# The first loads of a two-block transformer kernel issued early, in halves and in order, and the second block's context loaded and prepared sooner

## What is computed

```python
h = rms_norm(x, gain)
proj = jnp.einsum('bsd,de->bse', h, w_in)          # 1024 -> 9808 columns
...                                                 # three attentions: oa, ob, oc, each 512 wide
y = jnp.einsum('nbsw,nwd->bsnd', jnp.stack([oa, ob, oc], axis=0), w_branch)
gates = jax.nn.sigmoid(merge_logit).reshape(B, S, N_BRANCH, D_MODEL)
merged = jnp.sum(gates * y, axis=2)
return x + jnp.einsum('bsd,de->bse', merged, w_out)
```

```python
h   = modulate(x,   norm1_g[layer], sh1, sc1)
h_c = modulate(ctx, norm1_g[layer], csh1, csc1)
y = even_mixer(h, ...)         # layer 0; the same for h_c
...                            # layer 1: neighbourhood attention of x over x and ctx
x = x + g1 * y
x = x + g2 * conv_ffn(modulate(x, norm2_g[layer], sh2, sc2), ...)
```

## Time and profile before

| what | value |
|---|---|
| median of 3 runs | 1578.64 us (1578.16 to 1579.22) |
| the profiled execution | 1579.09 us, its span 1577.3 us |
| PE busy | 1538.7 us, 98% of the span |
| DVE, ACT, POOL busy | 66%, 48%, 6% |
| mean granted TensorE clock | 0.995 |
| moved by DMA | 260.9 MB, mean 165 GB/s |

### The profile page before, as it was taken

The page is one execution under the profiler, slowest core; times in us unless marked ns, Lnnn a source line. Parts: engine busy times, 40 slices in busy tenths (PEclk is TensorE's granted clock), DMA queues, the critical chain, the costliest instruction groups (busy, mean ns, idle before and its releaser), DMA issues.

```text
span 1577.3 us, 31432 instructions
## 1 busy us (share of the span) xinstructions
PE 1538.7 (98%) x13599; PEld 1472.3 (93%) x13599; DVE 1039.6 (66%) x1347; ACT 756.5 (48%) x1132; POOL 100.7 (6%) x79
## 2 busy tenths in 40 slices
PE   5999999999999999999999999999999999989999
PEld 5999999999999999899999999999999996889999
DVE  5878767578877775554456758886345347766674
ACT  4555554465465544653355322233245327655453
POOL 0311000003010000000020000000011002000000
PEclk9999999999999999999999999999999999989999
DMA  7676454566774546512035557754335224245854
GB/s 263 217 242 221 163 178 149 183 228 208 241 241 160 188 161 211 178 64 81 28 108 174 174 180 241 243 179 143 90 116 174 90 81 102 86 134 154 234 172 136
DMA packets 312333, 260.92 MB, mean 165 GB/s; under 512 B 24066, under 2 KB 298498, under 8 KB 312068
## 3 DMA queue, kind: packets, MB, share of 16 engines
q1 hardware_dynamic: 294260, 253.52, 49.6%
q10 hardware_dynamic: 17936, 5.40, 1.6%
HBM read 257.85 MB, written 1.05 MB: 164 GB/s over the span
## 4 chain that ended last, share of the span: by engine, by line
PE 54%; issue 7%; DVE 5%; ACT 3%; DMA 0%; POOL 0%; ACTq 0%; DVEq 0%; SPq 0%; POOLq 0%
PE banks_g L1417 34%; PE banks_g L967 7%; PE banks_g L1127 5%; PE banks_g L1276 2%; DVE w_lo L2498 1%; ACT near_p L2043 1%; DVE w_lo L2200 1%; PE banks_g L956 1%; ACT w_hi L1794 1%; PE banks_g L1378 1%; PE bank_s L1450 0%; POOL bias L2128 0%; PE bank_t L1464 0%; DVE near_max L2792 0%; PE bank_t L894 0%
## 5 line engine op out<-in xcount | busy, mean ns | idle before, releaser
L1417 PE MATMUL banks_g<-h_hi,w_lo 128*128 128x256 f32 x1296 | 360.5, 278 | 1.0 <-DVE w_lo L2498 0.6
L1417 PE MATMUL banks_g<-h_lo,w_hi 128*128 128x256 f32 x1296 | 358.5, 277 | 0.0
L1417 PE MATMUL banks_g<-h_hi,w_hi 128*128 128x256 f32 x1296 | 358.5, 277 | 0.0
L2498 DVE TENSOR_TENSOR w_lo<-raw,w_hi 128x2048 fp32r<-128x2048 f32 (+1 forms) x100 | 207.6, 2076 | 100.6 <-ACT w_hi L1794 100.3
L2200 DVE TENSOR_TENSOR w_lo<-raw,w_hi 128x2048 fp32r<-128x2048 f32 x92 | 212.4, 2310 | 72.5 <-ACT w_hi L1594 72.2
L1417 PEld LDWEIGHTS banks_g<-h_hi,w_lo 128*128 128x128 f32 x1296 | 243.5, 188 | 3.0 <-issue 0.9
L1417 PEld LDWEIGHTS banks_g<-h_hi,w_hi 128*128 128x128 f32 x1296 | 243.6, 188 | 0.0
L1417 PEld LDWEIGHTS banks_g<-h_lo,w_hi 128*128 128x128 f32 x1296 | 243.3, 188 | 0.1
L967 PE MATMUL banks_g<-h_hi,w_lo 128*128 128x256 f32 x800 | 226.0, 283 | 0.3 <-DVE w_lo L2200 0.3
L967 PE MATMUL banks_g<-h_hi,w_hi 128*128 128x256 f32 x800 | 221.4, 277 | 0.0
L967 PE MATMUL banks_g<-h_lo,w_hi 128*128 128x256 f32 x800 | 221.4, 277 | 0.0
(11 more groups left out here) (414 smaller groups left out, 3277.3 us busy)
## 6 DMA issues: line engine op xcount, KB each, us to landing
raw<-w_in SPq DMA_DIRECT2D x76, 1024.0 KB, 4.8
raw<-w_up SPq DMA_DIRECT2D x88, 512.0 KB, 4.9
ada_raw<-ada_w SPq DMA_DIRECT2D x24, 1024.0 KB, 7.1
raw<-w_down SPq DMA_DIRECT2D x32, 704.0 KB, 4.3
raw<-w_branch SPq DMA_DIRECT2D x12, 1024.0 KB, 4.9
ada_raw<-ada_t SPq DMA_DIRECT2D x12, 1024.0 KB, 4.9
late_raw<-ada_t SPq DMA_DIRECT2D x12, 1024.0 KB, 5.0
raw<-qkv SPq DMA_DIRECT2D x12, 1024.0 KB, 4.9
```

Of the source, the lines that this page charges most:

```text
L1417: last = nc.tensor.matmul(to, w[:, c, m0:m0 + P], a[:, c, s_ * SEQ:s_ * SEQ + SEQ], start=(m, s_, c, n) == (0, 0, 0, 0), stop=(m, s_, c, n ...
L2498: nc.vector.tensor_tensor(w_lo[:, u % SLOTS, 0:n], raw[:, u % SLOTS, 0:n], w_hi[:, u % SLOTS, 0:n].bitcast(F32), ALU.subtract).then_inc(dv ...
```

## The change

At the start ACT issues `ident` and `vectors`, with a counter of their own. SP issues `x` in two halves by features, unit 0 in two halves by chunks, unit 1, `ada` 0, unit 2, `w_small`, the six constants and unit 3, and waits for nothing before these. ACT makes the small columns for `ada` (`s_f`, `s_cols`) first, then two banks of `o_hi`, half of unit 0, two banks, the other half, then the sums of squares of x by rows from `x_in` with its accumulator, then unit 1. DVE reads the banks for `o_lo` itself, takes `w_lo` of unit 0 in two halves, and copies x to `x_t` afterwards. In layer 0 PE makes one matmul in place of the 8 of `sumsq`, and the root is taken from ACT's own sums. PE starts unit 0 on the first half of `w_lo`.

In the last layer SP issues `c_in` in two halves with units 40 and 41, the first behind a wait for PE's step `values15`; the other constants come with unit 2 of `END`. `ctx prep` 0 moves to after unit 39, 1 to after 41, 2 and 3 to after 42 and 43, ahead of the `merged` items there. The other lines of the diff change counts and pass the source of `o_lo`.

```diff
@@ -254,13 +254,17 @@
...
         if n in (42, 43):
+            order.append(("ctx prep", n - 40))
             order += [("merged", 2 * (n - 42)), ("merged", 2 * (n - 42) + 1)]
...
             order.append(("sums", n - 44))
-        order.extend(("ctx prep", m) for m, at in enumerate((41, 44, 44, 45)) if n == at)
+        if n == 39:
+            order.append(("ctx prep", 0))
+        if n == 41:
+            order.append(("ctx prep", 1))
...
-            sp.dma_start(ident[:, :], ins["ident"]).then_inc(x_loaded, 16)
-            sp.dma_start(vec_in, ins["vectors"].rearrange("(a p) f -> p a f", p=P)).then_inc(x_loaded, 16)
-            sp.dma_start(x_in, ins["x"][0].rearrange("(t p) f -> p t f", p=P)).then_inc(x_loaded, 16)
+            for n in range(2):
+                sp.dma_start(x_in[:, :, n * 512:n * 512 + 512],
+                             ins["x"][0].rearrange("(t p) f -> p t f", p=P)[:, :, n * 512:n * 512 + 512]
+                             ).then_inc(x_loaded[n], 16)
...
-                    sp.wait_ge(pe_steps, pe_.at(f"unit{before}", before=u < SLOTS))
-                    sp.sem_inc(sp_passed, 1)
+                    if layer or u >= SLOTS:
+                        sp.wait_ge(pe_steps, pe_.at(f"unit{before}", before=u < SLOTS))
+                        sp.sem_inc(sp_passed, 1)
...
                             src = columns(section * WIDTH + i * 256, 256)
+                    if (layer, u) == (0, 0):
+                        sp.dma_start(dst[:, 0:KC // 2, :], src[:, 0:KC // 2, :]).then_inc(half_loaded, 16)
+                        dst, src = dst[:, KC // 2:KC, :], src[:, KC // 2:KC, :]
                     sp.dma_start(dst, src).then_inc(raw_loaded[u % SLOTS], 16)
-                    if u == 41 and layer == DEPTH - 1:
-                        sp.dma_start(c_in[:, :, :], ins["ctx"][0].rearrange("(t p) f -> p t f", p=P)
-                                     ).then_inc(ctx_loaded, 16)
-                        sp.dma_start(dft_c[:, :], ins["dft_c"]).then_inc(end_loaded, 16)
-                        sp.dma_start(dft_t[:, :, :, :], ins["dft_t"]).then_inc(end_loaded, 16)
-                        sp.dma_start(w_s[:, :, :], ins["w_s"].rearrange("g p q -> p g q")).then_inc(end_loaded, 16)
-                        for r in (0, 32):
-                            sp.dma_start(b_s[r:r + 1, :, :], ins["b_s"].rearrange("(o g) p -> o g p", o=1)
-                                         ).then_inc(end_loaded, 16)
+                    if u in (40, 41) and layer == DEPTH - 1:
+                        t = u - 40
+                        if t == 0:
+                            sp.wait_ge(pe_steps, pe_.at("values15"))
+                        sp.dma_start(c_in[:, t, :], ins["ctx"][0, t * P:t * P + P, :]).then_inc(ctx_loaded[t], 16)
+                    if u == (1 if layer else 2):
+                        if layer:
+                            sp.wait_ge(pe_steps, pe_.at("small", before=True))
                         sp.dma_start(w_small[:, :, :], columns(K_IDX0, 80)).then_inc(small_loaded, 16)
+                        if layer == 0:
+                            for dst, src in ((rope[:, :, :], ins["rope"]), (causal[:, :, :], ins["causal"]),
+                                             (upto[:, :, :], ins["upto"]), (pick[:, :], ins["pick"]),
+                                             (add_parts[:, :], ins["add_parts"]),
...
+                                sp.dma_start(dst, src).then_inc(consts_loaded, 16)
...
+                        if u == (1 if (layer, n) == (0, 0) else min(slot_n + 2, len(UNITS) - 1)):
+                            if layer or n:
+                                sp.wait_ge(pe_steps, pe_.at(f"ada{(n - 1) % PACK}", before=n == 0))
+                                sp.sem_inc(sp_passed, 1)
                             sp.dma_start(ada_raw[:, :].rearrange("p (c n) -> p c n", c=KC),
                                          ada_columns(*divmod(layer * PACK + n, MOD_UNITS))).then_inc(ada_loaded, 16)
...
                 sp.dma_start(dst, src).then_inc(raw_loaded[u % SLOTS], 16)
+                if u == 2:
+                    sp.dma_start(w_s[:, :, :], ins["w_s"].rearrange("g p q -> p g q")).then_inc(end_loaded, 16)
+                    for r in (0, 32):
+                        sp.dma_start(b_s[r:r + 1, :, :], ins["b_s"].rearrange("(o g) p -> o g p", o=1)
+                                     ).then_inc(end_loaded, 16)
+                    sp.dma_start(dft_c[:, :], ins["dft_c"]).then_inc(end_loaded, 16)
+                    sp.dma_start(dft_t[:, :, :, :], ins["dft_t"]).then_inc(end_loaded, 16)
...
-            pe.wait_ge(x_loaded, 16 * 3)
...
             for b in range(4):
+                if b % 2 == 0:
+                    pe.wait_ge(x_loaded[b // 2], 16)
...
+                if layer == 0:
+                    pe.wait_ge(act_steps, act_.at("vec"))
+                    nc.tensor.matmul(bank_t[:, 0, 0:1], ones[:, :], ones[:, 0:1], start=True, stop=True
+                                     ).then_inc(pe_steps, pe_.step("sumsq"))
+                    return
...
-                        if u < AHEAD:
+                        if (layer, u) == (0, 0):
+                            pe.wait_ge(half_lo, 1)
+                        elif u < AHEAD:
...
                                     if u == 0:
                                         pe.wait_ge(x_gained, layer * KC + (c + 1))
+                                        if (layer, c) == (0, KC // 2):
+                                            pe.wait_ge(first_lo, 1)
...
-            act.dma_start(rope[:, :, :], ins["rope"]).then_inc(consts_loaded, 16)
-            act.dma_start(causal[:, :, :], ins["causal"]).then_inc(consts_loaded, 16)
...
+            act.dma_start(ident[:, :], ins["ident"]).then_inc(vec_loaded, 16)
+            act.dma_start(vec_in, ins["vectors"].rearrange("(a p) f -> p a f", p=P)).then_inc(vec_loaded, 16)
...
             act.wait_ge(act_steps, act_.last())
+            cc = vec[:, ROWS["c"]:ROWS["c"] + 16].rearrange("p (s c) -> p s c", s=2)
+            nc.scalar.activation(s_f[:, :, :], cc, ACT.Tanh, scale=0.5).then_inc(act_steps, act_.step("s tanh"))
+            act.wait_ge(pool_steps, pool_.at("s cols"))
+            act.wait_ge(dve_start, 1)
+            for s in range(2):
+                nc.scalar.activation(s_cols[:, :, S_AT + s], s_f[:, s, :], ACT.Copy, scale=0.5
+                                     ).then_inc(act_steps, act_.step("s cols"))
...
                                          ).then_inc(act_steps, act_.step(f"x hi{c}"))
-                if b % 2 == 0:
-                    act.wait_ge(raw_loaded[b // 2], 16)
-                    nc.scalar.activation(w_hi[:, b // 2, :], raw[:, b // 2, :], ACT.Copy
-                                         ).then_inc(act_steps, act_.step(f"hi{b // 2}"))
-            cc = vec[:, ROWS["c"]:ROWS["c"] + 16].rearrange("p (s c) -> p s c", s=2)
-            nc.scalar.activation(s_f[:, :, :], cc, ACT.Tanh, scale=0.5).then_inc(act_steps, act_.step("s tanh"))
-            for i in range(4):
-                act.wait_ge(dve_start, i + 1)
-                squares(i)
-            act.wait_ge(pool_steps, pool_.at("s cols"))
-            act.wait_ge(dve_start, 5)
-            for s in range(2):
-                nc.scalar.activation(s_cols[:, :, S_AT + s], s_f[:, s, :], ACT.Copy, scale=0.5
-                                     ).then_inc(act_steps, act_.step("s cols"))
+                if b % 2:
+                    n = b // 2
+                    act.wait_ge(raw_loaded[0] if n else half_loaded, 16)
+                    half = slice(n * UNIT // 2, (n + 1) * UNIT // 2)
+                    nc.scalar.activation(w_hi[:, 0, half], raw[:, 0, half], ACT.Copy
+                                         ).then_inc(act_steps, act_.step(f"first hi{n}"))
+            for t in range(2):
+                nc.scalar.activation(qk[0][:, 4 * t:4 * t + 4, :].rearrange("p a t -> p (a t)"), x_in[:, t, :],
+                                     ACT.Square, accum_out=token_root1[:, t:t + 1]
+                                     ).then_inc(act_steps, act_.step("x rows"))
+            act.wait_ge(raw_loaded[1], 16)
+            nc.scalar.activation(w_hi[:, 1, :], raw[:, 1, :], ACT.Copy).then_inc(act_steps, act_.step("hi1"))
...
+                        else:
+                            act.wait_ge(act_steps, act_.at("x rows"))
+                        nc.scalar.activation(token_root1[:, :], bank_o[:, SUM_COL:SUM_COL + 2] if layer else
+                                             token_root1[:, :], ACT.Sqrt,
...
-            for b in range(4):
-                dve.wait_ge(act_steps, act_.at(f"x hi{2 * b + 1}"))
-                nc.vector.tensor_copy(x_t[:, 2 * b:2 * b + 2, :], x_banks[b]).then_inc(dve_start, 1)
-                dve.wait_ge(dve_start, b + 1)
-                for c in (2 * b, 2 * b + 1):
-                    x_low(c, vec[:, n:n + KC])
-                if b == 0:
-                    first_low(0)
...
```

(26 more changed lines are left out.)

49 lines of the change are left out of this document (22 added, 27 removed).

## The result

The changed kernel takes **1570.17 us** (median; 1569.03 to 1573.88), the kernel before, on the same chip, 1578.93 (1578.16 to 1579.84): a ratio of 0.9948, 95% interval [0.993, 0.9967]. It is 8.8 us faster where 12.4 were forecast, 0.2 us outside the range. The profiled execution spans 1567.5 us against 1577.3, 9.8 less, to set against the 12.2 of the forecast's sum.

The account below looks back on a forecast made before the run. PE, busy 98% of the span, was taken as the bound. Gains of 10.9 us at the start and 1.3 at the last layer's end sum to 12.2: 1579.09 to 1566.9, forecast as median 1566.5, range 1562.5 to 1570.

Parts of the forecast that it names:

- t0: Kernel start: the time the vectors land, taken as 4.5 us, between 3.7 and 5.4.
- Part 1: Kernel start: PE can start unit 0 at 10.8 to 10.9 us, not at 20.71.
- ACT's chain: Kernel start: the steps from the vectors' landing to PE's start of unit 0, 6.3 us in sum.
- Part 2: From unit 0 to unit 1: 8.8 us instead of 9.87, unit 1 starting at 19.7, gain 10.9 us.
- Part 3: Layer 0: later loads, constants and splits stay hidden under PE's work, the constants with 5 us of cover.
- Part 4: Last layer's end: unit 47 split 3.1 us sooner, last add at 666.9 instead of 668.21, gain 1.3 us.
- The sum: Whole kernel: 10.9 + 1.3 = 12.2 us off the profiled 1579.09, giving 1566.9; forecast median 1566.5.
- rival A: Unit 0: the clock is already high, but unit 1 waits for `w_lo`; only 1.1 us more, 1565.4; chance 0.2.
- B: Start: loads on one queue share the rate instead of queueing; unit 1 starts at 25, 1571.7 us; chance 0.06.
- C: Last layer's end: something else holds the second block, so no gain there; 1567.8 us; chance 0.1.
- D: Last layer: slower, ACT stands at `ctx prep` 0 for the context load; over 0.2% if landing after 639; chance 0.01.
- E: Start: early loads don't move PE's start; only the end and 1 us of sums gain, 1576.4 us; chance 0.03.

Follow-up runs that it names:

- experiment 2: The change with `ident` and the vectors issued by SP ahead of x instead of by ACT: 1574.2 us, ratio 0.9971 to the kernel before.
- experiment 6: experiment 2 with PE's sums over `logf` one unit later, behind unit 4 and the first scores: 1571.01 us, ratio 0.9945.
- experiment 7: The change plus matmuls of ones, 14 before the vectors' wait, 5 behind the transposes: 1569.61 us; with edits of experiments 2 and 6, 8 and none: 1570.12 us.
- experiment 9: experiment 2 with 8 matmuls of ones ahead and the six constants behind unit 3, sums over `logf` at their old place: 1567.27 us, ratio 0.9918.
- experiment 11: experiment 8 with `ident` and the vectors issued by SP between the halves of x, 10 matmuls of ones instead of 14: 1568.8 us, ratio 0.992.
- experiment 5: The change with SP waiting for the vectors, still issued by ACT, before issuing the first unit's weights: 1574.91 us, ratio 0.9967.
- experiment 3: Only the start of the change, with the last layer's end as in the kernel before: 1573.8 us, ratio 0.9968.
- experiment 4: Only the last layer's end of the change, applied to the kernel before with its old start: 1575.97 us, ratio 0.9986.
- experiment 10: The change with the six constants asked for behind unit 3 and nothing else: 1569.24 us, ratio 0.9928.
- experiment 8: experiment 7's first kernel (14 and 5 matmuls of ones) with the six constants asked for behind unit 3: 1566.03 us, ratio 0.9911.

## Why the prediction was wrong

The direction, the place of the gain and the mechanism held in the change; two terms of the start were too large, one at the end too small, and what was called hidden in layer 0 was hidden only because the start came later than forecast.

**Landing of the vectors, t0 (Part 1): failed.** "So they land between 3.7 and 5.4; I take t0 = 4.5". They landed at 7.35, outside my own bounds, 2.9 us. I had the row of `rope` on the same queue, but beside it stood 0.25 MB on SP's queue and x came later, in the change 1 MB of x and then weights. Order of issue counts as well: 2.5 to 2.6 us when first (experiments 2, 6 and 7) and 3.7 once (9), 4.5 between the halves of x (11), 5.5 beside x alone (5), 5.7 to 6.2 beside x and the weights. The forecast even held the rule for it: the Trainium skill, "DMA: Bandwidth & Descriptors", section "Issuing engines are not separate DMA queues", says that loads from several engines interleave on the same DMA engines. These rows agree, and I was wrong to write that it leaves the sum as it is.

**ACT's chain: right.** From the vectors to unit 0 in 13.38 - 7.38 = 6.0 us, forecast 6.3. The forecasts for x (4.9 and 6.2, measured 4.9 and 6.5) and the weights, which ACT never waited for up to unit 2, held too. Unit 3 landed at 23.84, 1.0 later than forecast, behind constants that moved at 335 to 360 GB/s and not at 386.

**Unit 0 to unit 1 (Part 2): 9.8 instead of 8.8.** The term kept the slow matmuls of the earlier trace rows, which I had read as 21 at 0.21 us; counted as in the change, by the distance to the next, they are 19. There were 27, so eight more at 0.1 us, 0.8 in all. The other 0.1 to 0.2: one matmul in place of the 8 of `sumsq` gave 0.87, not 1.0. Both starts together: 10.9 - 2.9 + 0.3 - 1.0 = 7.3, measured 7.4.

**Layer 0 hidden (Part 3): right in the change, wrong for the start that I forecast.** In the change PE has no new wait up to the last layer. But with the lead at 10.3 to 11.5 us at 36 us instead of 7.4, and the constants where the change has them, experiments 2, 3 and 7 show waits of 3.40, 1.34 and 1.63 for `logf`; I had forecast 10.9. Even with the constants moved, experiments 9 and 11 show 0.87 and 1.45. The clock fell with the waits of 2, 5 and 11, and not with those of 3, 7 and 9. I had judged the constants by when they are read themselves, and not by what their 2 us in SP's queue do to unit 3 behind them; and I followed `w_lo` to the next unit, but not the small chain through `w_f`, ACT's two table loads and `logf`, on which PE's sums wait. So a landing at 4.5 would not have given the 12.2 either.

**The end (Part 4): 2.1 instead of 1.3.** The mechanism was right: the last add waits for PE alone. I set it at PE's old end, 666.9, without the 0.6 us that PE itself gains there in the same paragraph (0.28 wait and 0.3 restart). PE gained 1.0 net by then: 0.6 from that, 0.4 from the wait for `h` at 639.89, which the forecast didn't have and which is gone in experiment 4 too, so by the moved preparation of the context, 0.4 from the slower pace of the kernel before in this execution, less 0.35 lost between layer 0 and unit 40.

**The sum:** 12.2 - 2.9 + 0.3 - 1.0 + 0.8 = 9.4, measured 9.8 in the profiled execution. The median lies one more us from that, which is scatter of the runs (1569.03 to 1573.88). (The range's low end takes off 1.2 us for which no row is named; it is near the 1.1 of rival A.)

**Rivals.** *A*, the high clock at unit 0, did not happen in the two profiled executions of the change, but did in experiments 2, 3, 5 and 6, whose PE has nothing but transposes before unit 0 either. In experiment 10 the clock rose as well, within the transposes, at 10.0 us, fell again at 13.4 and rose at 16.8. Four of seven, or five, is far from my 0.2, and whether a given launch has it is not a property of the kernel. It is worth 2.7 us at 36 us (10.3 in experiment 3 against 7.4 to 7.7) and 1.1 or less behind `logf`: my price of 1.1 was right by another wait than the one I named. The Trainium skill, "TensorE: Matmul & The Clock Gate", "Part 4: PE-mode transpose", says that transposes don't count for the clock. These starts contradict it: in experiments 2, 3, 5 and 6 the record of the granted clock has the rise at 10.3 to 12.1 us, before the first matmul of unit 0. In experiment 4, whose start is that of the kernel before, it stands in the rows, within the transposes (the earlier ones come 0.21 us apart, the last four take 0.60 us together where the kernel before took 1.06):

```profile
9.30 0.90 PE L870 MATMUL bank_t<-ident,qk 128*128 128x128 f32 x3 [9.30 <-DMA h<-x]
...
12.54 0.60 PE L877 MATMUL bank_m<-ident,h 128*128 128x128 f32 x4
```

The change and its repetition went the other way: no rise before 19.3 us. *B*, loads that share: not at the unit's weights, but between x and the vectors, as above, and once in one queue: in experiment 8 `rope`, issued 2.6 us behind unit 3, landed at 22.16, before unit 3's 22.75. "One queue serves its loads in order" was too strong. *C* fell (2.1 us at the end). *D* fell: ACT has the context's squares at 614.15 without idling for the load. *E* fell.

## What to carry to other kernels

When a start is pulled forward, follow every load to what stands behind it in the queue, not only to its own reader: 0.78 MB of constants that nobody needed yet held up one unit's weights by 2 us, and moving them was worth 2.1 us in the rows (2.7 in the medians, with intervals that overlap) once PE came early, and nothing that can be seen before. A small load that opens the chain goes ahead of the large ones; here it took 2.5 to 3.7 us so, and 5.5 to 6.2 beside 1 MB asked for at the same moment by another engine. Cover is to be counted against the start that is forecast, through the small chains too, since a wait on TensorE can cost as much again in the low clock behind it: 3.2, 4.4 and 1.9 us behind waits of 3.40, 3.92 and 1.45 (experiments 2, 5 and 11), though under 1 us behind 1.34 and 1.63 (3 and 7).

## What was not expected of the hardware

- A load of 192 KB took 2.6, 4.5, 5.5 or 6.1 us by what else was in flight (experiments 2, 11, 5 and the change); the same arrangement scatters, 2.5 to 3.7 us when first (2, 6, 7 and 9).
- The pace of unit 0 behind the same transposes was 0.21 us for 27, 15 or none of its 48 matmuls, in kernels with the same start (the change, experiments 10 and 3). The clock can rise within transposes alone (experiments 4 and 10). What decides it stays open. With matmuls of ones ahead it was high in experiments 7, 8 and 11, and low for 14 matmuls in 9.
- In experiment 11 the clock fell at 45.1 us, 1.5 us after a wait of only 1.45 us had ended at 43.64; waits of 1.34 and 1.63 had no such fall.
- A 4% slower pace, 0.118 us a matmul instead of 0.113, with the granted clock shown as 1.00 and PE without a wait: in stretches in every execution, and from 1460 us to the end in experiment 3.
